# Triangular inverse of a chunked RWKV-7 layer: the level of 32 as 32 by 32 products, the last level in two column halves

## What is computed

```python
def step(S, inp):
    r_t, w_t, k_t, v_t, a_t, b_t = inp
    sa = jnp.einsum('bhij,bhj->bhi', S, a_t)
    S = S * w_t[:, :, None, :] + sa[..., None] * b_t[:, :, None, :] + v_t[..., None] * k_t[:, :, None, :]
    y_t = jnp.einsum('bhij,bhj->bhi', S, r_t)
    return S, y_t
```

## Time and profile before

| what | value |
|---|---|
| median of 3 runs | 1474.78 us |
| lowest and highest run | 1473.46 and 1477.78 us |
| span of the profiled execution, first to last instruction | 1471.8 us |
| instructions in the span | 34271 |
| VectorE busy | 691.5 us (47%) |
| ScalarE busy | 514.4 us (35%) |
| GpSimd busy | 579.4 us (39%) |
| mean granted TensorE clock | 0.997 of 2.4 GHz |
| all DMA queues | 143.08 MB |

### The profile page before, as it was taken

The page is one execution under the profiler, slowest core; times in us unless marked ns, Lnnn a source line. Parts: engine busy times, 40 slices in busy tenths (PEclk is TensorE's granted clock), DMA queues, the critical chain, the costliest instruction groups (busy, mean ns, idle before and its releaser), DMA issues.

```text
span 1471.8 us, 34271 instructions
## 1 busy us (share of the span) xinstructions
PE 1432.0 (97%) x14670; PEld 1344.3 (91%) x14670; DVE 691.5 (47%) x1447; ACT 514.4 (35%) x856; POOL 579.4 (39%) x740
## 2 busy tenths in 40 slices
PE   4999999999999999999999999999999999899998
PEld 4998999999999899999999999989999899699998
DVE  7117475664847557475664435343353444500000
ACT  6233242422514233242422544434444343322221
POOL 6353241422424134241422434434344443954442
PEclk9999999999999999999999999999999999999999
DMA  5333131311313113131311853735537375345361
GB/s 198 84 91 89 35 94 37 82 53 45 89 38 84 44 45 104 26 98 38 83 52 38 204 134 90 166 94 144 129 95 166 93 170 127 131 130 158 102 165 45
DMA packets 252084, 143.08 MB, mean 97 GB/s; under 512 B 12109, under 2 KB 245006, under 8 KB 251406
## 3 DMA queue, kind: packets, MB, share of 16 engines
q1 hardware_dynamic: 228316, 125.90, 33.6%
q10 hardware_dynamic: 23618, 15.00, 3.5%
HBM read 125.36 MB, written 15.45 MB: 96 GB/s over the span
## 4 chain that ended last, share of the span: by engine, by line
PE 85%; DVE 4%; POOL 3%; ACT 1%; issue 1%; ACTq 0%; DVEq 0%; POOLq 0%
PE acc L483 57%; PE head_banks L929 3%; PE head_banks L934 3%; PE head_banks L919 2%; PE head_banks L871 2%; PE head_banks L1077 1%; PE head_banks L1097 1%; POOL XL L764 1%; PE head_banks L997 1%; PE head_banks L1090 1%; PE head_banks L1046 1%; PE head_banks L986 1%; PE head_banks L838 1%; PE head_banks L967 1%; PE head_banks L886 1%
## 5 line engine op out<-in xcount | busy, mean ns | idle before, releaser
L466 POOL TENSOR_TENSOR WL<-WR,WH 128x256 fp32r<-128x256 f32 (+1 forms) x656 | 507.1, 804 | 858.9 <-ACT WH L456 838.5
L483 PE MATMUL acc<-XH,WH 128*128 128x260 f32 (+1 forms) x2624 | 569.4, 298 | 9.5 <-POOL WL L466 6.9
L483 PE MATMUL acc<-XH,WL 128*128 128x260 f32 (+1 forms) x2624 | 528.5, 283 | 0.0
L483 PE MATMUL acc<-XL,WH 128*128 128x260 f32 (+1 forms) x2624 | 527.7, 283 | 0.0
L483 PEld LDWEIGHTS acc<-XH,WH 128*128 128x128 f32 (+1 forms) x2624 | 404.6, 188 | 39.9 <-issue 28.7
L483 PEld LDWEIGHTS acc<-XL,WH 128*128 128x128 f32 (+1 forms) x2624 | 404.3, 188 | 0.0
L483 PEld LDWEIGHTS acc<-XH,WL 128*128 128x128 f32 (+1 forms) x2624 | 403.7, 188 | 0.0
L456 ACT ACTIVATE WH<-WR 128x1024 fp32r<-128x1024 f32 (+1 forms) x164 | 171.5, 1048 | 121.9 <-PE acc L483 114.6
L491 ACT ACTIVATE AREN<-acc 128x520 f32<-128x520 f32 (+1 forms) x82 | 49.4, 603 | 362.1 <-PE acc L483 354.8
L1929 DVE TENSOR_TENSOR AREN<-head_banks,AREN 128x512 f32<-128x512 f32 x16 | 11.1, 692 | 169.1 <-PE head_banks L1148 169.1
L1723 DVE TENSOR_TENSOR AREN<-AREN,head_banks 128x128 f32<-128x128 f32 x160 | 46.3, 289 | 33.3 <-PE head_banks L929 19.0
(11 more groups left out here) (238 smaller groups left out, 1597.5 us busy)
## 6 DMA issues: line engine op xcount, KB each, us to landing
WR<-in_w_in SPq DMA_DIRECT2D x128, 512.0 KB, 4.1
WR<-in_w_out SPq DMA_DIRECT2D x32, 512.0 KB, 6.9
out<-AREN ACTq DMA_DIRECT2D x32, 256.0 KB, 3.2
AREN<-in_cache_k_win SPq DMA_DIRECT2D x16, 384.0 KB, 8.0
AREN<-in_cache_v_win SPq DMA_DIRECT2D x16, 384.0 KB, 8.9
mix_scratch<-AREN ACTq DMA_DIRECT2D x16, 260.0 KB, 4.2
AREN<-in_x_prompt SPq DMA_DIRECT2D x4, 1024.0 KB, 7.6
AREN<-in_cache_k_win SPq DMA_DIRECT2D x8, 512.0 KB, 6.9
```

What stands on the lines that cost most here:

```text
L466: rest = pool.tensor_tensor(WL[:, place, j:j + 2, 0:M], WR[:, k % 4, j:j + 2, 0:M], WH[:, place, j:j + 2, 0:M].bitcast(F32), ALU.subtract)
L483: mm = pe.matmul(acc[0:M, hf, 0:HT], w[:, (4 * g + k) % 3, j, 0:M], x[:, kt, hf * HT:(hf + 1) * HT], start=(kt == 0 and n == 0), stop=(kt ...
```

## The change

The loop over levels ends at level 4, and level 5 (blocks of 32) is written out. Its `qt` takes only the 32 by 32 block below the diagonal (`NN[second, q, first]` by `XT[second, q, 32:64]`), so no mask is needed, and a plain copy brings it out of PSUM. `dy` and `dx` are 32 by 32 products too, and `dx` is formed for the upper block of 64 only. Per pair that is 16 + 16 + 8 products of 32 by 32 in place of 16 + 16 + 16 of 64 by 64. ScalarE makes both copies of `XT` into `XTF` after level 4, ahead of level 5's results; the transposed corrections of level 5 go straight to `XTF`, one quadrant by ScalarE (new steps `oa`, `ob`) and one by VectorE, which waits for `fa` or `fb` there. The last level reads `XTF[low, q, low]`. Its products go by turns to rows 0 to 63 and 64 to 127 of PSUM (`BLOCKS[q % 2]`), 128 columns each, and each copy out of PSUM becomes two, of which the second reads partitions 64 to 127 and writes 0 to 63. TensorE waits for `oa` ahead of `qt6b`, and for `q6b` ahead of the chunk loop.

```diff
--- before.py
+++ after.py
@@ -387,7 +387,7 @@
                       f"y{NC - 1}", "st", "mean", "var"])
         ACT_A = Steps(["ksq", "sgw", "sga", "sgg", "tail", "e1", "e2", "ln", "rn", "g", "dcs", "vec",
                        "nn01", "tokb", "tokk", "tokv", "nn23",
-                       "fa", "q6b", "fb",
+                       "fa", "fb", "oa", "ob", "q6b",
                        *[f"{s}{c}" for c in range(NC) for s in ("rhs", "u")],
                        "st", "y", "ysq", "yln", "yrs"])
         DVE_M = Steps(["par", "dsh", "dss", "mix"], ahead=False)
@@ -520,6 +520,7 @@
             return a.rearrange("p q (n u m) -> p q n u m", u=2, m=m)[:, :, :, which, :]
 
         BLOCKS = (slice(0, 64), slice(64, 128))
+        HALVES = ((slice(0, 32), slice(32, 64)), (slice(64, 96), slice(96, 128)))
 
         def four(h):
 
@@ -906,7 +907,7 @@
                 transposed_n(2, 3, "nn23")
 
 
-                for l in range(1, last):
+                for l in range(1, last - 1):
                     for h, bank in (("a", 0), ("b", 2)):
                         if l == 1:
                             pe.wait_ge(a_act, ACT_A.at(i, "nn23"))
@@ -935,13 +936,37 @@
                                                half_of(X[k, q, :], l, 0), start=True, stop=True)
                         mm.then_inc(a_pe, PE_A.one(f"dx{l}{h}"))
                     fill(f"dx{l}b")
+                for h, bank in (("a", 0), ("b", 2)):
+                    pe.wait_ge(a_dve, DVE_A.at(i, f"x{last - 2}{h}"))
+                    pe.sem_inc(s_passed, 1)
+                    for q in each(h):
+                        for first, second in HALVES:
+                            mm = pe.matmul(HB[first, bank, (q % 4) * 32:(q % 4 + 1) * 32], NN[second, q, first],
+                                           XT[second, q, 32:64], start=True, stop=True)
+                    mm.then_inc(a_pe, PE_A.one(f"qt{last - 1}{h}"))
+                for h, bank_y, bank_x in (("a", 1, 0), ("b", 3, 2)):
+                    pe.wait_ge(a_dve, DVE_A.at(i, f"q{last - 1}{h}"))
+                    pe.sem_inc(s_passed, 1)
+                    for q in each(h):
+                        for first, second in HALVES:
+                            mm = pe.matmul(HB[first, bank_y, (q % 4) * 32:(q % 4 + 1) * 32], X[first, q, 0:32],
+                                           QT[first, q, 0:32], start=True, stop=True)
+                    mm.then_inc(a_pe, PE_A.one(f"dy{last - 1}{h}"))
+                    first, second = HALVES[0]
+                    for q in each(h):
+                        mm = pe.matmul(HB[second, bank_x, (q % 4) * 32:(q % 4 + 1) * 32], QT[first, q, 0:32],
+                                       X[first, q, 0:32], start=True, stop=True)
+                    mm.then_inc(a_pe, PE_A.one(f"dx{last - 1}{h}"))
+                fill(f"dx{last - 1}b")
                 top, low = BLOCKS
                 for h, bank in (("a", 0), ("b", 1)):
                     pe.wait_ge(a_dve, DVE_A.at(i, f"x{last - 1}{h}"))
+                    if h == "b":
+                        pe.wait_ge(a_act, ACT_A.at(i, "oa"))
                     pe.sem_inc(s_passed, 1)
                     for q in each(h):
-                        mm = pe.matmul(HB[top, bank, (q % 4) * 64:(q % 4 + 1) * 64], NN[low, q, top], XT[low, q, :],
-                                       start=True, stop=True)
+                        mm = pe.matmul(HB[BLOCKS[q % 2], bank, (q % 4 // 2) * 64:(q % 4 // 2 + 1) * 64], NN[low, q, top],
+                                       XTF[low, q, low], start=True, stop=True)
                     mm.then_inc(a_pe, PE_A.one(f"qt{last}{h}"))
                     fill(f"qt{last}{h}")
                 for h, bank in (("a", 2), ("b", 3)):
@@ -951,8 +976,8 @@
                         pe.wait_ge(a_act, ACT_A.at(i, "q6b"))
                     pe.sem_inc(s_passed, 1)
                     for q in each(h):
-                        mm = pe.matmul(HB[top, bank, (q % 4) * 64:(q % 4 + 1) * 64], X[top, q, :], QT[top, q, :],
-                                       start=True, stop=True)
+                        mm = pe.matmul(HB[BLOCKS[q % 2], bank, (q % 4 // 2) * 64:(q % 4 // 2 + 1) * 64], X[top, q, :],
+                                       QT[top, q, :], start=True, stop=True)
                     mm.then_inc(a_pe, PE_A.one(f"dx{last}{h}"))
                     fill(f"dx{last}{h}")
 
@@ -975,6 +1000,7 @@
                     if c == 0:
                         pe.wait_ge(a_dve, DVE_A.at(i, "xf6b"))
                         pe.wait_ge(a_pool, POOL_A.at(i, "zf"))
+                        pe.wait_ge(a_act, ACT_A.at(i, "q6b"))
                     else:
                         pe.wait_ge(a_dve, DVE_A.at(i, f"s{c - 1}"))
                         pe.wait_ge(a_act, ACT_A.at(i, f"rhs{c - 1}"))
@@ -1297,21 +1323,29 @@
                 act.dma_start(RV.rearrange("p a b -> p (a b)"),
                               vec_d[i].rearrange("b h v k -> (b h) (v k)").unsqueeze(1).to_broadcast([16, 8, 6 * HD]))\
                    .then_inc(s_rv, 16)
-                for l in range(1, last):
+                for l in range(1, last - 1):
                     feed(f"dx{l}b")
 
                 def whole(h):
                     act.wait_ge(a_pool, POOL_A.at(i, "zf"))
-                    act.wait_ge(a_dve, DVE_A.at(i, f"xt{last - 1}{h}"))
+                    act.wait_ge(a_dve, DVE_A.at(i, f"xt{last - 2}{h}"))
                     for k in BLOCKS:
                         full = act.activation(XTF[k, four(h), k], XT[k, four(h), :], ACT.Copy)
                     full.then_inc(a_act, ACT_A.one(f"f{h}"))
 
                 whole("a")
+                whole("b")
+                feed(f"dx{last - 1}b")
+                for h, bank in (("a", 1), ("b", 3)):
+                    act.wait_ge(a_pe, PE_A.at(i, f"dy{last - 1}{h}"))
+                    act.wait_ge(a_act, ACT_A.at(i, f"f{h}"))
+                    act.activation(XTF[0:32, four(h), 32:64], HB[0:32, bank, 0:128].rearrange("p (q t) -> p q t", q=4),
+                                   ACT.Copy, scale=-1.0).then_inc(a_act, ACT_A.one(f"o{h}"))
                 act.wait_ge(a_pe, PE_A.at(i, "qt6b"))
-                act.activation(QT[0:64, 4:8, :].rearrange("p a b -> p (a b)"), HB[0:64, 1, 0:256], ACT.Copy)\
-                   .then_inc(a_act, ACT_A.one("q6b"))
-                whole("b")
+                for k, block in enumerate(BLOCKS):
+                    low_q = act.activation(QT[0:64, 4 + k:8:2, :], HB[block, 1, 0:128].rearrange("p (q t) -> p q t", q=2),
+                                           ACT.Copy)
+                low_q.then_inc(a_act, ACT_A.one("q6b"))
                 for s in ("qt6b", "dx6b"):
                     feed(s)
                 for c in range(NC):
@@ -1723,12 +1757,29 @@
                             dve.tensor_tensor(part, part, HB[:, bank, 0:128].rearrange("p (q n m) -> p q n m", q=4, m=2 ** l),
                                               ALU.subtract).then_inc(a_dve, DVE_A.one(f"{to}{l}{h}"))
                 quarter = lambda a: a.rearrange("p (q t) -> p q t", q=4)
+                for h, bank in (("a", 0), ("b", 2)):
+                    dve.wait_ge(a_pe, PE_A.at(i, f"qt{last - 1}{h}"))
+                    dve.tensor_copy(QT[:, four(h), 0:32], quarter(HB[:, bank, 0:128]))\
+                       .then_inc(a_dve, DVE_A.one(f"q{last - 1}{h}"))
+                for h, bank_y, bank_x in (("a", 1, 0), ("b", 3, 2)):
+                    dve.wait_ge(a_pe, PE_A.at(i, f"dy{last - 1}{h}"))
+                    dve.wait_ge(a_act, ACT_A.at(i, f"f{h}"))
+                    dve.tensor_scalar(XTF[64:96, four(h), 96:128], quarter(HB[64:96, bank_y, 0:128]), -1.0, None,
+                                      ALU.mult).then_inc(a_dve, DVE_A.one(f"xt{last - 1}{h}"))
+                    dve.wait_ge(a_pe, PE_A.at(i, f"dx{last - 1}{h}"))
+                    dve.tensor_scalar(X[32:64, four(h), 0:32], quarter(HB[32:64, bank_x, 0:128]), -1.0, None,
+                                      ALU.mult).then_inc(a_dve, DVE_A.one(f"x{last - 1}{h}"))
                 dve.wait_ge(a_pe, PE_A.at(i, "qt6a"))
-                dve.tensor_copy(QT[0:64, 0:4, :], quarter(HB[0:64, 0, 0:256])).then_inc(a_dve, DVE_A.one("q6a"))
+                for k, block in enumerate(BLOCKS):
+                    low_q = dve.tensor_copy(QT[0:64, k:4:2, :], HB[block, 0, 0:128].rearrange("p (q t) -> p q t", q=2))
+                low_q.then_inc(a_dve, DVE_A.one("q6a"))
                 for h, bank in (("a", 2), ("b", 3)):
                     dve.wait_ge(a_pe, PE_A.at(i, f"dx6{h}"))
-                    dve.tensor_scalar(XTF[0:64, four(h), 64:128], quarter(HB[0:64, bank, 0:256]), -1.0, None,
-                                      ALU.mult).then_inc(a_dve, DVE_A.one(f"xf6{h}"))
+                    for k, block in enumerate(BLOCKS):
+                        low_x = dve.tensor_scalar(XTF[0:64, four(h), :][:, k:4:2, 64:128],
```

(3 more changed lines are left out.)

## The result

The changed kernel takes 1480.74 us in the median of 19 runs (1475.58 to 1485.83), the kernel before 1477.68 us in as many beside it. The ratio over all these runs is 1.0033, with a 95% interval of 1.0022 to 1.0044: slower by a third of a percent, where 0.46% faster was forecast. (The two medians alone would give 1.0021: most runs of the kernel before lie either near 1474 or near 1478 us, and its median fell on the upper group.) The changed kernel's runs also scatter over 10 us, twice as far as before.

A forecast was written before the change was run, and what follows sets the result against it. TensorE, busy 97% of the span, was taken as the bound; level 32 has no fill behind it. Gaining 0.85 us a pair, 6.8 over eight, gives a median of 1468.0 from 1474.78, range 1463.5 to 1474.

The forecast's parts named there:

- Small products: Level 32's 32 by 32 products: 80 instructions instead of 96, at 0.029 us each, perhaps less.
- the 2.5 that was named as a sign: Sign of being right: ScalarE's XTF copies end by 2.5 us after the start of level 32.
- qt6a, qt6b, dx6a: Last level's products, in us from level 32's start: forecast 2.74, 3.30 and 4.54, before 2.97, 3.83 and 5.32.
- The column halves: Last level's products work side by side at 0.029 us: eight in 0.44 instead of 0.65, sixteen in 0.68.
- rival 1: Last level's column halves don't overlap weight loads: gain only 3.0 us, 1471.8; chance 0.28 together with double-priced shifted copies.
- The short copies: Last level's copies become two of 128 columns each: 0.57 for 0.42 us on DVE, no surcharge for shifted partitions.
- The gain on the path: Level 32's start to the chunk loop's first product takes 6.36 us instead of 7.23: 0.85 a pair, 6.8 in all.
- Behind L986 all of the pair moves together: After the chunk loop's first product, the rest of the pair moves earlier too, meeting no late weights from POOL.
- Rival 4: A wait later in the pair that nothing showed takes the gain back, leaving under 3 us; chance 0.04.
- my slower rival: Level 32's 32 by 32 tiles don't overlap, 0.058 us an instruction: 9 us lost, 1483.7; chance 0.06.
- The last of the signs of being wrong: Pairs shorter by 0.85 us in the inverse but not from one pair's start to the next.
- pairs which behave alike before go on doing so: The eight pairs behave alike, L943 waiting once in each, so what one gains counts eight times.

The follow-up runs named there:

- d_big: Changed kernel plus idle 128 by 128 by 260 products, three behind level 32 and two behind qt6a; 1474.52 us, 0.9985 of the kernel before.
- d_more: Changed kernel plus idle 128 by 128 by 260 products, four behind level 32 and three behind qt6a; 1470.03 us, 0.9968 of the kernel before.
- d_small: Changed kernel plus idle 32 by 32 by 32 products, 12 behind level 32 and 8 behind qt6a; 1478.20 us, 1.0018 of the kernel before.
- a_level32: Level 32 as in the changed kernel, last level as in the kernel before; 1496.65 us, 1.0140 of the kernel before.
- f_extra: Changed kernel with one unit of projection work moved from the pair's end to behind level 32; 1464.81 us, 0.9931 of the kernel before.
- e_wide: Changed kernel with level 32's 40 products in 64 by 64 tiles moving 32 columns, inverse not computed; 1476.78 us, 1.0016 of the kernel before.
- b_halves: Last level in column halves as in the changed kernel, level 32 as in the kernel before; 1474.44 us, 0.9987 of the kernel before.

## Why the prediction was wrong

Point by point, by its own steps:

- **Small products.** Taken at 0.029 an instruction, as the nearest rows; measured (0.73 - 0.19)/31 = 0.017 for L944. As it said, the faster rate bought nothing at once, because fb then holds xt5b: 335.38 is 2.41 after the start, forecast 2.54 to 2.58. ScalarE's four copies into XTF end at 2.31, inside the 2.5 that was named as a sign.
- **qt6a, qt6b, dx6a** were forecast at 2.74, 3.30 and 4.54 and came at 2.29, 3.16 and 4.45. The column halves were priced exactly. The rule of the Trainium skill, "TensorE: Matmul & The Clock Gate", Part 3, on weight loads of one row group, rival 1's ground, does not hold here: eight instructions on one row group and two column halves take 0.45.
- **The short copies** were 0.59 for two and 1.21 for four, forecast 0.57 and 1.18, with no surcharge for the shift of partitions.
- **The gain on the path**, 0.85 a pair, was right: 0.95 in the first pair of the changed kernel, and 88.5 to 87.7 in the pairs of d_big without a fall. L1012 came at 6.20 in the first pair, a little ahead of the forecast 6.36, because x5b was done at 3.01, not 3.15, and L1012 started 0.05 behind the last copy (it ends at 161.09), not 0.15. So PE waited 0.17 for that copy, not 0.37.
- **The step that failed** is "Behind L986 all of the pair moves together". It took for granted that the rows behind the change run at the clock of the trace before. They do not: seven pairs have a stretch at 0.50. A pair with it takes 88.7 in place of 87.7, and this 1.0 is more than the 0.85 that the change saves. The second pair, with a mean clock of 0.96, takes 90.45, 2.8 more. Six falls at 1.0 and one at 2.8 are 8.8 us against 6.8 saved, so 2.0 of the 2.9 us by which the span grew; the other 0.9 was not traced. No rival had this, and the range (to 1474.0) left no room for it. Rival 4, a gain taken back later in the pair, had the right place but named a wait; my slower rival (small tiles that don't overlap) was the wrong mechanism. The last of the signs of being wrong is the one that came: shorter by 0.8 in the inverse, but not from one pair's start to the next. The step before it failed with it, that pairs which behave alike before go on doing so: the first of the changed kernel has no fall and the others do.

What the traces offered: the clock was 1.00 in every pair before, and PE's standing still in that stretch was in all under half a microsecond. The change took TensorE's work out of the stretch and left the waits for DVE, so it became thinner in two ways, smaller products and longer waits. Big products put into the waits bring the clock back (d_more) and small ones do so less (d_small), so more than the standing still counts. Whether the tile size counts by itself, and how much, is not shown. The Trainium skill, "TensorE: Matmul & The Clock Gate", Part 1, describes a clock that is let down when TensorE has been idle; the traces agree that it is let down to half, but in the pairs of the changed kernel the longest standstill ahead of a fall is 0.46 us, in a stretch with products all around it.

What stays open is how the two weigh against each other, what part the time has at which the stretch comes around (the pair of a_level32 that kept the clock), and why the same kernel's executions differ by up to 10 us: with 0.987 of the clock the fastest takes 1475.58, and with 0.979 another takes 1484.6, so how often and how long the clock is down varies from run to run.

## What to carry to other kernels

A change that leaves TensorE less to do in a stretch has to be priced with the clock in it: look at what stays behind in the stretch, not only at what leaves it, and put dense work where products have become small. Here the same change was worth +0.3% without and -1.0% with one unit of six products moved, and that unit in its place was worth nothing to the kernel before. When a kernel's runs scatter more than those of the one before it, look at the granted clock by stretches; its mean over the whole span (0.986) looks harmless. And a unit of work taken from another place can open a wait there, as in f_extra.

## What the runs showed of the hardware

- TensorE instructions (two for each fp32 product) in 32 by 32 tiles that move 32 columns, two row strips in turn, start 0.017 us apart on average and last 0.19 (L944 of the changed kernel); in 64 by 64 tiles they start 0.029 apart and last 0.22 (L944 of e_wide).
- Two column halves of the same rows work side by side in fp32, weight loads included: 0.033 an instruction against 0.06. In b_halves eight weight loads of 0.13 each are over in 0.34.
- Instructions on tiles that don't overlap can start out of order: in the trace before, the first products of qt6a (155.04 + 2.97) start among the last ones of dx5b, which stand ahead of them in the program.
- The granted clock can fall to half although TensorE never stood still for more than 0.46 us ahead of it. In six pairs of the changed kernel such a fall lasts 3.4 us (mean clock of the pair 0.98), in a_level32, whose instructions of the last level stand nearly twice as far apart, 10.2 us (0.94).
- A copy of 64 partitions from PSUM partitions 64 to 127 to SBUF partitions 0 to 63 costs DVE 0.29 for 128 columns, within 0.01 of the unshifted one beside it (L1774 of the changed kernel, 283 to 295 ns).
